# Norm factors from column statistics and a diagonal, low parts three blocks behind, post-norms out of PSUM, attention's projections begun with the context

## What is computed

```python
def rms_norm(x, g):
    y = xf * lax.rsqrt(jnp.mean(xf * xf, axis=-1, keepdims=True) + RMS_EPS)
    return (y * g.astype(jnp.float32)).astype(x.dtype)

def modulate(h, shift, scale):
    return h * (1.0 + scale[:, None, :]) + shift[:, None, :]

h = modulate(rms_norm(x, norm1_g[l]), sh1, sc1)     # before mixer, attention, Fourier, feed-forward
x = x + g1 * rms_norm_2(y, norm_g[i, 1])            # post-norm, second block only
```

## Time and profile before

| | |
|---|---|
| Time, median of 3 runs (lowest, highest) | 2396.43 us (2394.58, 2398.36) |
| The profiled execution: its time, its span | 2398.32 us, 2396.5 us |
| Busy: PE, DVE, ACT, POOL | 90%, 42%, 28%, 11% of the span |
| HBM read | 654.70 MB, 274 GB/s over the span |

### The profile page before, as it was taken

One profiled execution on the slowest core, in us unless ns is written; L12 is line 12 of the kernel. 1 busy time (PEld: TensorE's weight loads), 2 busy tenths in 40 slices (PEclk: granted clock), 3 DMA queues, 4 the chain that ended last, 5 costly groups with the idle time before them and its releaser, 6 DMA issues.

```text
span 2396.5 us, 31356 instructions
## 1 busy us (share of the span) xinstructions
PE 2164.7 (90%) x13461; PEld 1541.3 (64%) x13461; DVE 1004.1 (42%) x1904; ACT 672.7 (28%) x1192; POOL 271.7 (11%) x116
## 2 busy tenths in 40 slices
PE   4998988999999989899899999998989799887998
PEld 2776674555555467777455555555756699866997
DVE  2465541111111136564221111112435677656776
ACT  2334421101111043343221111011023555434553
POOL 1453420000000044453000000000000000000000
PEclk7999989999999989999999999999999899998998
DMA  9865669999999966567799999997436365323550
GB/s 324 292 217 176 253 239 370 409 409 409 409 409 409 385 233 220 200 229 289 294 366 409 409 409 409 409 409 273 158 131 228 101 216 188 103 73 122 180 194 18
DMA packets 251189, 657.88 MB, mean 275 GB/s; under 512 B 16800, under 2 KB 129278, under 8 KB 238627
## 3 DMA queue, kind: packets, MB, share of 16 engines
q1 hardware_dynamic: 244032, 652.27, 72.0%
q10 hardware_dynamic: 7011, 3.53, 0.5%
HBM read 654.70 MB, written 1.06 MB: 274 GB/s over the span
## 4 chain that ended last, share of the span: by engine, by line
PE 83%; DVE 10%; ACT 3%; SPq 1%; issue 1%; DMA 1%; ACTq 0%
PE ps L407 82%; DVE AR L1898 2%; DVE AR L740 1%; DMA ring<-in_w_in 1%; SPq L340 1%; DVE AR L1945 1%; DVE xT L2515 1%; DVE hT L2513 1%; DVE XLr L802 1%; ACT AR L765 0%; ACT HBr L385 0%; ACT AR L726 0%; DVE ARr L1579 0%; DVE AR L793 0%; ACT hTr L774 0%
## 5 line engine op out<-in xcount | busy, mean ns | idle before, releaser
L407 PE MATMUL ps<-ring,AR 128*64 128x512 f32 (+1 forms) x2032 | 524.9, 580 | 33.1 <-DVE AR L1945 33.1
L407 PE MATMUL ps<-XLr,HBr 128*128 128x256 f32 x1408 | 417.8, 297 | 64.5 <-DVE XLr L802 44.9
L407 PE MATMUL ps<-AR 128*128 128x128 f32 (+6 forms) x2088 | 379.7, 344 | 14.0 <-DVE AR L1879 7.5
L407 PEld LDWEIGHTS ps<-ring,AR 128*64 128x64 f32 (+1 forms) x2032 | 203.1, 140 | 273.1 <-issue 266.7
L407 PE MATMUL ps<-hTr,ringr 128*128 128x256 f32 x1280 | 371.9, 291 | 0.0
L407 PE MATMUL ps<-hTr,HBr 128*128 128x256 f32 x1280 | 371.4, 290 | 0.0
L391 POOL TENSOR_TENSOR ringr<-ring,HBr 128x1024 fp32r<-128x1024 f32 x112 | 271.5, 2440 | 853.0 <-ACT HBr L385 853.0
L407 PEld LDWEIGHTS ps<-AR 128*128 128x128 f32 (+2 forms) x2088 | 288.8, 191 | 119.6 <-issue 76.9
L407 PEld LDWEIGHTS ps<-XLr,HBr 128*128 128x128 f32 x1408 | 279.1, 198 | 88.9 <-issue 38.8
L385 ACT ACTIVATE HBr<-ring 128x1024 fp32r<-128x1024 f32 x260 | 266.1, 1050 | 238.8 <-PE ps L407 211.2
L407 PEld LDWEIGHTS ps<-hTr,ringr 128*128 128x128 f32 x1280 | 256.0, 200 | 0.8 <-issue 0.5
(11 more groups left out here) (270 smaller groups left out, 2362.5 us busy)
## 6 DMA issues: line engine op xcount, KB each, us to landing
ring<-in_w_expert_in SPq DMA_DIRECT2D x154, 1024.0 KB, 15.2
ring<-in_w_expert_out SPq DMA_DIRECT2D x84, 1024.0 KB, 10.1
ring<-in_mod_w SPq DMA_DIRECT2D x48, 1024.0 KB, 6.6
ring<-in_ffn_w_up SPq DMA_DIRECT2D x44, 1024.0 KB, 5.7
ring<-in_w_in SPq DMA_DIRECT2D x40, 1024.0 KB, 5.5
ring<-in_w_ada SPq DMA_DIRECT2D x40, 1024.0 KB, 7.3
HB<-in_w_expert_in SPq DMA_DIRECT2D x36, 1024.0 KB, 14.5
XL<-in_w_expert_in SPq DMA_DIRECT2D x22, 1024.0 KB, 14.3
```

The source lines that it names most:

```text
L407: return pe.op.matmul(out_, lhsT, rhs, start=start, stop=stop, **kw)
```

## The change

- Statistics: the squares are now the stationary operand, against one column of 1/1024, so that two columns hold the means of the 256 tokens, one token a partition (`Rstd.pe_stats`). ACT takes the root of 128 x 2, DVE the reciprocal, and scales the identity matrix with it into a diagonal, 128 x 256 (`dve_diagonal`). PE multiplies ones with the diagonal (`pe_spread`): the factors then stand in a PSUM bank for all partitions.
- Apply: DVE multiplies x with the factors out of PSUM; the coefficient goes to ACT as the scale of "out". Low parts come three blocks behind the scale; in layer 0's first norm all scales come early, all low parts last.
- Post-norms read y in PSUM; the copies of y are gone. The factors are copied to SBUF first; the addition of block k - 1 follows the product of block k. During a post-norm the statistics take `hbank` or `bank`.
- `pe_heads` begins with the context's first projection, then statistics, the context's second projection, the spread, two modulation products, and the query projections, which wait block by block.
- ACT squares before it makes the last units of layer 1's first projection; two of these units move into the last pair of layer 0's experts. The DMA of that weight, and of attention's first two key and value weights, is issued before SP reads the flag. The order of slots is another, and the overflow block uses slots 2 to 7.
- The context's norm: statistics where the means were, the spread behind the pair's down products.

```diff
@@ -740,29 +741,74 @@
             dve.op.reciprocal(rs[:, 0:n], rs[:, 0:n]).then_inc(*dve_norm.inc(tag, "rstd"))
             dve.wait_ge(*dve_norm[tag, "rstd"])
+        class Rstd:
...
+            @property
+            def rs(self):
+                return self.banks["spread", self.tag][:, 0:256]
+            def pe_stats(self, pe):
+                pe.wait_ge(*self.banks.turn("norm", self.tag))
+                b = self.banks["norm", self.tag]
+                for k in range(8):
+                    pe.wait_ge(*act_norm[self.squared(k)])
+                    for j in range(2):
+                        a = k * 256 + j * 128
+                        t = mm(pe, b[:, j:j + 1], self.sq[:, a:a + 128], C("m1024", 0, 1), k == 0 and j == 0, k == 7,
+                               skip_group_check=True)
+                t.then_inc(*pe_norm.inc(self.tag, "mean"))
+                self.banks.until(("norm", self.tag), act_norm, self.tag, "root")
+            def act_root(self, act):
+                act.wait_ge(*pe_norm[self.tag, "mean"])
+                act.op.activation(self.st, self.banks["norm", self.tag][:, 0:2], ACT.Sqrt,
+                                  bias=eps[:, 0:1]).then_inc(*act_norm.inc(self.tag, "root"))
+            def dve_diagonal(self, dve):
+                dve.wait_ge(*act_norm[self.tag, "root"])
+                dve.op.reciprocal(self.st, self.st).then_inc(*dve_norm.inc())
+                dve.wait_ge(*dve_norm.now())
+                for j in range(2):
+                    dve.op.tensor_scalar(diag[:, j * 128:(j + 1) * 128], ident, self.st[:, j:j + 1], None,
+                                         ALU.mult).then_inc(*dve_norm.inc(self.tag, "diagonal"))
+            def pe_spread(self, pe):
+                pe.wait_ge(*self.banks.turn("spread", self.tag))
+                pe.wait_ge(*q_cst0["all"])
+                pe.wait_ge(*dve_norm[self.tag, "diagonal"])
+                mm(pe, self.rs, C("ones"), diag[:, :], True, True).then_inc(*pe_norm.inc(self.tag, "spread"))
+                self.banks.until(("spread", self.tag), *self.until)
         class NormMod:
...
+            def act_stats(self, act):
                 act_squares(act, self.tag, lambda k: self.src[:, sl(k)], 8, 256, self.sq, self.ready)
-                act_root(act, self.tag, 256, self.rs)
-                if self.tag == ("n1", 0):
-                    act_small(act)
-                    act_units(act, ahead(("qk", 0, 0, 0)))
-                    act.wait_ge(*q_scr["all"])
-                self.act_apply(act)
+                self.r.act_root(act)
             def act_apply(self, act):
+                act.wait_ge(*dve_norm[self.tag, "coef"])
                 for k in range(8):
                     act.wait_ge(*dve_norm[self.tag, "scaled", k])
-                    act.wait_ge(*dve_mod[self.mod])
-                    act.op.activation(self.full[:, sl(k)], self.full[:, sl(k)], ACT.Identity,
+                    act.op.activation(self.full[:, sl(k)], self.full[:, sl(k)], ACT.Identity, scale=self.coef[:, k:k + 1],
                                       bias=self.shift[:, k:k + 1]).then_inc(*act_norm.inc(self.tag, "out", k))
                     if self.split and k:
...
@@ -774,28 +820,33 @@
                 act.op.activation(XH[:, sl(k)], self.sq[:, sl(k)], ACT.Copy).then_inc(*act_norm.inc(self.tag, "high", k))
...
+                for k in range(5, 8) if self.split else ():
+                    self.dve_low(dve, k)
+            def dve_scale(self, dve, low=True):
+                dve.wait_ge(*pe_norm[self.tag, "spread"])
                 for k in range(8):
-                    dve.op.scalar_tensor_tensor(self.full[:, sl(k)], self.src[:, sl(k)], self.coef[:, k:k + 1], self.rs,
-                                                ALU.mult, ALU.mult).then_inc(*dve_norm.inc(self.tag, "scaled", k))
-                    if self.split and k:
-                        self.dve_low(dve, k - 1)
-                if self.split:
-                    self.dve_low(dve, 7)
+                    dve.op.tensor_tensor(self.full[:, sl(k)], self.src[:, sl(k)], self.r.rs,
+                                         ALU.mult).then_inc(*dve_norm.inc(self.tag, "scaled", k))
+                    if self.split and low and k >= 3:
+                        self.dve_low(dve, k - 3)
...
-                return dve_norm[self.tag, "low", k] if self.split else act_norm[self.tag, "out", 7]
+                return dve_norm[self.tag, "low", k] if self.split else act_norm[self.tag, "out", k]
...
@@ -1622,7 +1674,8 @@
             W1, W2 = A["w_expert_in"][l], A["w_expert_out"][l]
-            all_ = ((8, 9, 10, 7, 5, 6, 0, 1, 2, 3, 4, 12, 13), (8, 9, 11, 6, 7, 5, 0, 1, 2, 3, 12, 13, 4))[l]
+            all_ = ((8, 9, 10, 7, 5, 6, 1, 2, 3, 4, 0, 12, 13), (8, 9, 11, 6, 7, 5, 2, 3, 12, 13, 0, 1, 4))[l]
...
@@ -1633,6 +1686,11 @@
                                 sp.wait_ge(*pe_unit["o", l, 3, 1])
                             load(sp, (which, l, e, n), by_rows(W[e, n * 256:(n + 1) * 256, :]), 2, 1024, all_)
                             n_load += 1
+            if l == 0:
+                sp_mixer_first(sp, 1)
+            else:
+                sp_kv(sp, 0)
...
@@ -2003,9 +2061,11 @@
                 if p + 1 < NE // 2:
                     pe_gather(pe, l, m, p + 1)
                 if (l, p) == (1, 1):
-                    normC.pe(pe)
+                    normC.r.pe_stats(pe)
                 pe_turn(pe, l, m, p)
                 pe_down(pe, l, m, p)
+                if (l, p) == (1, 1):
+                    normC.r.pe_spread(pe)
...
@@ -2016,13 +2076,15 @@
             act_gather(act, l, m, 0)
             for p in range(NE // 2):
                 act_up(act, l, m, p)
+                if (l, p) == (0, NE // 2 - 1):
+                    act_units(act, place.get(("qk", 1, 0, 1), 0) + 1)
                 if p + 1 < NE // 2:
                     act_gather(act, l, m, p + 1)
                 act_down(act, l, m, p)
                 if (l, p) == (1, 0):
                     act_squares(act, "ctx", lambda k: hcT[:, sl(k)], 8, 256, normC.sq, normC.ready)
                 if (l, p) == (1, 1):
-                    act_root(act, "ctx", 256, normC.rs)
+                    normC.r.act_root(act)
                 if (l, p) == (1, 2):
                     normC.act_apply(act)
...
@@ -2292,21 +2358,24 @@
             m.tmp.until(("r", i, g), dve_att, "roped", i, g)
         def pe_heads(pe, m, norm):
-            pe.wait_ge(*norm.done(7))
             pe.wait_ge(*act_norm["ctx", "out", 7])
-            pe_projq(pe, 0, 0)
-            pe_projq(pe, 0, 1)
-            pe_projkv(pe, 0, 0)
+            pe_projkv_half(pe, 0, 0, 0)
+            norm.r.pe_stats(pe)
+            pe_projkv_half(pe, 0, 0, 1)
+            norm.r.pe_spread(pe)
+            pe_mods(pe, 2)
+            pe_projq(pe, 0, 0, norm)
+            pe_projq(pe, 0, 1, norm)
             pe_hnorm(pe, m, 0, 0)
             pe_projkv(pe, 0, 1)
             pe_hnorm(pe, m, 0, 1)
...
@@ -2319,9 +2388,11 @@
             pe_mods(pe, 1)
             pe_rope(pe, m, 3, 1)
-        def act_heads(act, m):
+        def act_heads(act, m, norm):
+            norm.act_stats(act)
+            act_projkv(act, m, 0, 0)
+            norm.act_apply(act)
             act_hsquare(act, m, 0, 0)
...
@@ -2333,10 +2404,13 @@
             act_projkv(act, m, 1, 0)
             act_projkv(act, m, 1, 1)
-        def dve_heads(dve, m):
+        def dve_heads(dve, m, norm):
+            norm.dve_coef(dve)
+            dve_projkv(dve, m, 0, 0)
+            norm.r.dve_diagonal(dve)
+            norm.dve_apply(dve, 2)
             dve_projq(dve, m, 0, 0)
             dve_projq(dve, m, 0, 1)
-            dve_projkv(dve, m, 0, 0)
             dve_hnorm(dve, m, 0, 0)
             dve_projkv(dve, m, 0, 1)
...
@@ -2484,35 +2558,45 @@
         def dve_out(dve, l, hi, src):
             dve_halves(dve, ("out", l), hi, XL, src)
             for g in range(4):
-                dve_units(dve, ahead(("out", l, g, 0), 1))
-                dve.wait_ge(*pe_unit["out", l, g, 1])
-                dve.op.tensor_copy(hT[:, sl(g, 512)], bank["out", l, g][:, :]).then_inc(*dve_ffn.inc("y", l, g))
-                dve_units(dve, ahead(("out", l, g, 1), 1))
+                for m in range(2):
+                    dve_units(dve, ahead(("out", l, g, m), 1))
         class PostNorm:
...
             def act(self, act):
-                act_squares(act, self.tag, lambda k: hT[:, sl(k)], 8, 256, self.sq, self.ready)
-                act_root(act, self.tag, 256, self.rs)
+                for p in range(4):
+                    act.wait_ge(*self.summed(p))
+                    act.op.activation(self.sq[:, sl(p, 512)], self.y(p)[:, :], ACT.Square).then_inc(*act_norm.inc(self.tag, "sq", p))
+                self.r.act_root(act)
             def pe(self, pe):
-                pe_means(pe, self.tag, "m1024", 8, 256, self.sq)
+                self.r.pe_stats(pe)
+                self.r.pe_spread(pe)
```

(27 more changed lines are left out.)

146 lines of the change are left out of this document (78 added, 68 removed).

## The result

The changed kernel takes 2378.89 us (median, 2376.33 to 2381.15) against 2397.22 for the one before: ratio 0.9925, interval 0.9908 to 0.9942. It is faster, but by 18 us and not by the 44 of the forecast, whose range ended at 2374. The profiled execution took 2379.52 for a span of 2377.7.

A forecast was written before the change was run, and what follows sets the result against it. PE was taken as the bound (83% of the chain), with gains where it stands still or runs at 1.2 GHz. Terms 7.8 + 8.0 - 0.9 + 6.5 + 9.2 + 2.3 + 9.2 + 2.0 = 44.1 gave 2352, range 2335 to 2374.

The forecast's parts named there:

- The small steps: In each norm: 32 column statistics instructions cost 3.55 us at full clock, saving nothing on PE; root to first scale saves 1.0.
- the second rival: Column statistics leave PE at 1.2 GHz, costing 7.1 us a norm instead of 3.55: 22 back, 2374; chance 0.08.
- the rival of products that cost next to nothing: Column products almost free, squares and table load end last: heads save 3.5 more, six places 0.5 each, 2346; chance 0.02.
- Loops: Split norms: PE unbroken 6.45 us after the first scale instead of 12.46, 6.0 saved, plus 1.0 for the clock.
- First norm: Layer 0's first norm: PE past its eighth group's start by 55.8 instead of 61.79, plus 1.8 of cold running: 7.8 saved.
- Layer 1's norm and the context's: Norm before layer 1's mixer saves 8.0 us; context's norm loses 0.9, its spread waiting on PE before the next pair.
- Attention's start: From layer 1's scatter through the heads: context projections around the statistics, 10.0 us after against 16.5 before, 6.5 saved.
- Post-norm plus split norm: Two places, 9.2 us saved each: first scale 2.2 earlier, 6.0 from the loop, 1.0 from the clock.
- Fourier: Post-norm plus Fourier's norm: 2.3 us saved up to the scale; the eight outs take 3.3 before and after.
- Last post-norm: At the kernel's end: copies 0.7 us earlier, chain 0.4, loop 0.9, together 2.0 saved.
- Slower weights, a late slot: Rival in the expert stretch: reordered slots make weights late, 2414 at 2 us a pair; chance 0.03 for slower.
- a stopped loop: Rival: the loop stays one block at a time, four loops save nothing, nor the clock: 29 back, 2381; chance 0.08.

The follow-up runs named there:

- the second profile: The changed kernel itself, unedited, measured and profiled again: 2377.14 us, 0.9905; the profiled execution was the 2388.4.
- the wide kernel: The changed kernel with each statistics product 128 columns wide instead of one, all else kept: 2357.2 us, ratio 0.9825.

## Why the prediction was wrong, and where it was right

The direction was right, the size less than half. **The step that failed** is in "The small steps" and in the second rival: that the 32 column products of a norm cost 3.55 us, because they run at the full clock and leave it up for the work behind them. The runs showed 3.8 to 7.0 us in the seven norms behind attention, with the granted clock falling to 0.50 while they ran, and the same instructions with 128 columns brought the time down by 21.7 us. The price of one was right at both levels (0.11 and 0.22 us: 3.63 for 32 in the heads of the second profile, 6.96 before feed-forward 0), which also settles the rival of products that cost next to nothing; the clock was not. The forecast held a row of eight such products, 1.03 us long, against the rival "the column statistics leave PE at 1.2 GHz", and gave it 0.08. That row is too short to show what 3.5 to 7 us of them do. The rival's price was 22 us and its time 2374; the two kernels differ by 21.7. Its mechanism was right, but that the price fits so well is in part luck: it charged most of it to the statistics themselves, 3.55 us in each of five norms, while the statistics of the seven norms behind attention took 41.7 us in sum for 33.0 with wide ones, 8.7 of the 15.7 between the two kernels behind the heads. The rest stands in other work of that stretch. It should have had a chance of the forecast's own order, as nothing in the trace showed a long run of such products.

**Loops.** Forecast 6.45 us from first scale to the unbroken run; measured 7.22 before both feed-forward parts and 8.14 (847.07 to 855.21) before layer 1's mixer, the 6.45 only with the factor back on DVE (6.54). ACT needs 0.80 a block, not 0.71: the shift with its factor takes 0.59, which I had priced by rows without a factor. The 0.9 more in layer 1 is the low part beside POOL, which I had not seen; with POOL's work moved away it is 7.22 there too.

**First norm** (7.8): the unbroken run starts 9.9 earlier (51.94 for 61.79), 8.3 are left through the mixer's first half and 6.8 at its experts. **Layer 1's norm and the context's** (8.0 and -0.9): together 5.8, inside the bounds; the spread waits 3.09 us before the third pair, where the root's wait was 2.5.

**Attention's start** (6.5): 2.3 in the first profile, because the second projection took 10.04 instead of 7.07, the first 0.8 and the statistics 0.5 more than counted. In the second profile it is 5.8 (84.5 for 90.3), with wide statistics 7.1. So part of the missing 4.2 belongs to that one execution. The idle of 3.7 was predicted, and its cause held. The 4.8 then lost in attention itself, in both profiles, I had at nothing: the granted clock of this stage is 0.93 in the mean, for 0.97 before. Wide statistics leave 1.5 of it, at 0.96.

**Post-norm plus split norm** (9.2 each): 5.7 and 7.0, with wide statistics 9.4 and 9.2. The first scale was to come 2.2 us earlier; counted from the first root it came 1.0 later (13.97 for 12.95), for the statistics ended last and at the low clock. **Fourier** (2.3): -4.5, with wide ones 1.5; its eight shifts take 4.04 instead of 3.30, which the forecast had as equal. **Last post-norm** (2.0): 0.6, and 1.1.

Five microseconds are left between the wide kernel and the forecast. By the table they are 1.6 in the first norm, 1.0 in layer 1's and the context's, 1.5 in attention, 0.8 in the Fourier stage and 0.9 at the end, less 0.6 and 0.2 more won in the heads and in feed-forward 0. The shifts' factor costs about 0.7 in each of five places by their rows, but it is not shown to be these five microseconds: both feed-forward stages met their term with it, and moving it back gained nothing. What the others are stays open. Slower weights, a late slot or a stopped loop were not seen: the experts' pairs kept 30.3 us.

## What to carry to other kernels

When a change swaps wide products for narrow ones, cost them at both levels of TensorE's clock, and cost the work behind them at both, before trusting a price per instruction taken from a short run. If the narrow ones cost the same to load as wide ones, issue them wide and read one column. Take a part alone: here a few lines carried more than the whole. And profile the same kernel twice before reading a difference of a few microseconds in one stage as the work of an edit.

## What the runs showed of the hardware that I had not expected

The profile's busy share does not tell whether the clock stays up: 6.84 of 7 us busy with one-column products at 0.50, 3.67 of 4 us with 128 columns at 1.00. The Trainium skill, "TensorE: Matmul & The Clock Gate", section "What's actually happening", says that the clock follows how busy PE has been; by the busy column of this profile these two windows come out the other way round, and the measurement decides.

The clock can fall in the same products in one execution and not in the other. In the mixer of layer 0, behind an idle of 1.7 us each time; the kernel before, then the changed one:

```profile
193.03 2.52 PE L407 MATMUL ps<-AR 128*128 128x128 f32 x16
195.48 3.70 PE L407 MATMUL ps<-biasB,cst 128*128 128x512 f32 x8
```

```profile
184.70 4.24 PE L408 MATMUL ps<-AR 128*128 128x128 f32 x16
188.86 5.14 PE L408 MATMUL ps<-biasB,cst 128*128 128x512 f32 x8
```

That is 3.2 us for the same products. In the run with fillers around one-column statistics, whose code is that of the changed kernel up to the end of attention, the sixteen products took 2.52 us again and the clock stayed up until 207.5 us, so the code of this layer does not decide it. It is the size at which single stages of these kernels stop being comparable.
